# A two-layer encoder trunk: where a filter's spectrum is unfolded, and where its tap sums are multiplied

## The reference

```python
h_full = jnp.concatenate([h[:, 0], zeros((1, n_ch)), h[1:, 1][::-1]], axis=0)
h_full = h_full / jnp.sum(jnp.abs(h_full), axis=0, keepdims=True)
return jnp.fft.rfft(h_full, axis=0).reshape(L + 1, HY_ORDER, W_B)
...
for n, gate in enumerate((x1, x2)):
    z_f = jnp.fft.rfft(z, n=2 * L, axis=1)
    conv = jnp.fft.irfft(z_f * filt_f[:, n], n=2 * L, axis=1)[:, :L]
    z = gate * (conv + bias[n] * z)
```

## Time and profile before

| | |
|---|---|
| median of 3 runs | 2689.77 us (2687.35 to 2689.95) |
| profiled execution | 2684.76 us, of which 2683.2 us are the span |
| PE busy | 2596.8 us (97% of the span) |
| DVE busy | 1862.0 us (69%) |
| ACT busy | 1288.6 us (48%) |
| granted TensorE clock, mean | 0.987 |

### The profile page before, as it was taken

The page is one execution under the profiler, slowest core; times in us unless marked ns, Lnnn a source line. Parts: engine busy times, 40 slices in busy tenths (PEclk is TensorE's granted clock), DMA queues, the critical chain, the costliest instruction groups (busy, mean ns, idle before and its releaser), DMA issues.

```text
span 2683.2 us, 41615 instructions
## 1 busy us (share of the span) xinstructions
PE 2596.8 (97%) x13736; PEld 2157.6 (80%) x13736; DVE 1862.0 (69%) x3251; ACT 1288.6 (48%) x2334; POOL 111.6 (4%) x206
## 2 busy tenths in 40 slices
PE   7999999999999999999989999999999999999998
PEld 6889999976776768898778999898877767688986
DVE  7788778735776767556678878876367757765666
ACT  5555555543444334443465555556344433344535
POOL 2100000000000000000021000000000000000000
PEclk9999999999999999999999999999999999999998
DMA  7544444434443324555564444443344533355554
GB/s 250 164 147 152 152 145 148 157 114 150 150 163 124 128 96 163 187 175 172 165 205 154 152 146 151 148 151 131 138 145 151 173 102 126 102 187 187 173 172 144
DMA packets 115956, 411.83 MB, mean 153 GB/s; under 512 B 15460, under 2 KB 15514, under 8 KB 115584
## 3 DMA queue, kind: packets, MB, share of 16 engines
q1 hardware_dynamic: 107424, 391.17, 43.8%
q0 software_dynamic: 8416, 19.18, 2.2%
HBM read 403.99 MB, written 6.29 MB: 153 GB/s over the span
## 4 chain that ended last, share of the span: by engine, by line
PE 91%; DVE 4%; issue 2%; ACT 2%; DMA 1%; PEldq 0%; PEld 0%; DVEq 0%; POOL 0%; POOLq 0%; ACTq 0%
PE bank L1620 29%; PE bank L1660 19%; PE bank L1662 10%; PE bank L2000 6%; PE bank L1577 5%; PE bank L1595 4%; PE bank L1750 2%; PE bank L1732 2%; PE bank L1713 2%; PE bank L1920 2%; PE bank L1934 1%; PE bank L1818 1%; PE bank L1698 1%; PE bank L1900 1%; PE bank L1842 1%
## 5 line engine op out<-in xcount | busy, mean ns | idle before, releaser
L381 ACT ACTIVATE WH<-ring 128x512 fp32r<-128x512 f32 x1364 | 854.8, 631 | 1176.4 <-PE bank L1620 515.3
L395 DVE TENSOR_TENSOR WL<-ring,WH 128x512 fp32r<-128x512 f32 x852 | 573.3, 688 | 456.2 <-ACT WH L381 454.1
L1660 PE MATMUL bank<-XX,WH 128*128 128x512 f32 x2304 | 820.9, 400 | 27.7 <-DVE XX L564 15.4
L1662 PE MATMUL bank<-XX,WL 128*128 128x256 f32 x2304 | 644.5, 280 | 0.0
L1660 PEld LDWEIGHTS bank<-XX,WH 128*128 128x128 f32 x2304 | 435.7, 189 | 128.5 <-DVE XX L564 15.4
L1620 PE MATMUL bank<-WH,XX 128*128 128x512 f32 x1536 | 493.0, 402 | 4.4 <-issue 3.5
L386 DVE TENSOR_TENSOR WL<-ring,WH 128x512 fp32r<-128x512 f32 x512 | 350.5, 687 | 138.1 <-ACT WH L381 134.0
L1662 PEld LDWEIGHTS bank<-XX,WL 128*128 128x128 f32 x2304 | 437.4, 190 | 0.0
L1620 PEld LDWEIGHTS bank<-WH,XX 128*128 128x128 f32 x1536 | 290.1, 191 | 83.1 <-issue 22.4
L1620 PE MATMUL bank<-WL,XX 128*128 128x512 f32 x768 | 303.6, 395 | 0.0
L1620 PEld LDWEIGHTS bank<-WL,XX 128*128 128x128 f32 x768 | 146.6, 191 | 31.8
(11 more groups left out here) (311 smaller groups left out, 3340.3 us busy)
## 6 DMA issues: line engine op xcount, KB each, us to landing
ring<-in_blocks SPq DMA_DIRECT2D x738, 512.0 KB, 3.3
ARENA<-in_bc POOLq DMA_DIRECT2D x2, 2048.0 KB, 8.6
ARENA<-in_decay POOLq DMA_DIRECT2D x8, 512.0 KB, 4.0
ARENA<-in_x SPq DMA_DIRECT2D x4, 512.0 KB, 8.4
u_scratch<-ARENA POOLq DMA_DIRECT2D x16, 128.0 KB, 2.5
ARENA<-u_scratch POOLq DMA_DIRECT2D x64, 32.0 KB, 3.2
y_scratch<-ARENA POOLq DMA_DIRECT2D x16, 128.0 KB, 2.0
ARENA<-y_scratch POOLq DMA_DIRECT2D x64, 32.0 KB, 2.7
```

The costliest lines, as they stand in the source:

```text
L381: nc.scalar.activation(wh[q], raw(which[0], q), ACT.Copy).then_inc(wh_ready[q], 1)
L395: vec.tensor_tensor(wl[q], raw(which[0], q), wh[q].bitcast(F32), ALU.subtract).then_inc(w_used[slot(which[0], half)], 1)
L1660: ins = mm(bank[b][:, :], h, xx[:, :, k, :], start=(k == 0), stop=(k == DT - 1), skip_group_check=True)
L1662: ins = mm(bank[b][:, 0:T], l, xh[:, k, :], start=False, stop=(k == DT - 1), skip_group_check=True)
```

## The change

It does three things.

- `unfold` is moved on DVE, in slots 2 and 5, from behind the second half of the next block's low parts to between the halves.
- `tap_sums` is moved on PE from slot 8 (behind the forward transform) to slot 6, into the block itself, between its quarters 1 and 2, and writes bank 4 instead of bank 6. Bank 4 held the turned z just before, and holds the first forward transform just after.
- The reciprocal is moved on DVE from slot 8, ahead of the product, to slot 6, behind the second half of the low parts; it now frees bank 4.

```diff
-    "hyc":  [4, 4, 4, 4, 18, 18, 20, 18],
+    "hyc":  [4, 4, 4, 4, 20, 18, 18, 18],
...
-            at = {"taps": 2 * n, "dft": 2 * n + 1, "turn": 4, "fwd": 5 + n, "inv": 7 + n, "sums": 6}[step]
-            return o * 10 + at + (step == "inv" or step == "fwd" and n == 1) if b == 6 else o * 9 + at
+            at = {"taps": 2 * n, "dft": 2 * n + 1, "sums": 5, "turn": 4, "fwd": 5 + n, "inv": 7 + n}[step]
+            return o * 10 + at + (step in ("fwd", "inv")) if b == 4 else o * 9 + at
...
+                    if s_ in (2, 5):
+                        unfold(o, s_ // 3)
                     if s_ in (7, 8, 9):
-                        if s_ == 8:
-                            full(6, "hyc", hyc(o, "sums", 0, 6))
-                            free(v.reciprocal(NS[:, o * 8:o * 8 + 8], bank[6][:, 0:8]), 6)
                         product(o, (0, 1, 1)[s_ - 7], (0, 0, 1)[s_ - 7])
...
-                    if s_ in (2, 5):
-                        unfold(o, s_ // 3)
+                    if s_ == 6:
+                        full(4, "hyc", hyc(o, "sums", 0, 4))
+                        free(v.reciprocal(NS[:, o * 8:o * 8 + 8], bank[4][:, 0:8]), 4)
...
-                def token_block(b, x, j, n, *which):
+                def token_block(b, x, j, n, between, *which):
 
                     for q in range(4):
+                        if q == 2 and between is not None:
+                            between()
...
-                    take_bank(6, "hyc", hyc(o, "sums", 0, 6))
+                    take_bank(4, "hyc", hyc(o, "sums", 0, 4))
...
+                    between = None
                     if s_ == 6:
                         turn_z(o)
+                        between = lambda: tap_sums(o)
...
-                    if s_ == 8:
-                        tap_sums(o)
```

More of the change, by code:

```diff
@@ L356, in split_number, with hyc @@
             return layer * SPLITS + (block_ - skipped + 1) + turn * per
-        def hyc(o, step, n=0, b=4):
-            at = {"taps": 2 * n, "dft": 2 * n + 1, "turn": 4, "fwd": 5 + n, "inv": 7 + n, "sums": 6}[step]
-            return o * 10 + at + (step == "inv" or step == "fwd" and n == 1) if b == 6 else o * 9 + at
+        def hyc(o, step, n, b):
+            at = {"taps": 2 * n, "dft": 2 * n + 1, "sums": 5, "turn": 4, "fwd": 5 + n, "inv": 7 + n}[step]
+            return o * 10 + at + (step in ("fwd", "inv")) if b == 4 else o * 9 + at
         def lift_a(k):
@@ L468, in _ @@
                     if c:
-                        pool.wait_ge(psum_free[7], read_out(layer, "hyc", 7, hyc((c - 1) // 2, "taps", (c - 1) % 2)))
+                        pool.wait_ge(psum_free[7], read_out(layer, "hyc", 7, hyc((c - 1) // 2, "taps", (c - 1) % 2, 7)))
                     else:
@@ L480, in _ @@
                     elif c == 2:
-                        pool.wait_ge(psum_free[7], read_out(layer, "hyc", 7, hyc(0, "inv", 1)))
+                        pool.wait_ge(psum_free[7], read_out(layer, "hyc", 7, hyc(0, "inv", 1, 7)))
                     pool.sem_inc(dec_free, 1)
@@ L983, in even_odd @@
                 def even_odd(o, c):
-                    out_of(7, "hyc", hyc(o, "taps", c))
+                    out_of(7, "hyc", hyc(o, "taps", c, 7))
                     dve.wait_ge(taps_ready, layer * CHUNKS + (o * 2 + c + 1))
                     if c:
-                        full(7, "hyc", hyc(o, "dft", 0))
+                        full(7, "hyc", hyc(o, "dft", 0, 7))
                     f, b = HH[:, 0:2 * CW], HH[:, 2 * CW:4 * CW]
@@ L1637, in token_block, with gated_block @@
                             ins[1].then_inc(parts_used[q], 1)
-                def gated_block(stage, g, p, x, y, *which):
+                def gated_block(stage, g, p, x, y, *which, between=None):
                     b = 0 if p < 4 else 2
@@ L1644, in gated_block @@
                             take_bank(b + t, stage, g)
-                    token_block(b, y if b else x, p - 4 if b else p, 2 if b else 4, *which)
+                    token_block(b, y if b else x, p - 4 if b else p, 2 if b else 4, between, *which)
                 def wide_half(b, half, *which):
@@ L1886, in tap_sums @@
                     pe.wait_ge(sums_ready, layer * CHUNKS + (o * 2 + 2))
-                    take_bank(6, "hyc", hyc(o, "sums", 0, 6))
+                    take_bank(4, "hyc", hyc(o, "sums", 0, 4))
                     for j in range(8):
-                        ins = mm(bank[6][:, j:j + 1], SUM[:, j * P:(j + 1) * P], ones[:, 0:1], start=True, stop=True)
+                        ins = mm(bank[4][:, j:j + 1], SUM[:, j * P:(j + 1) * P], ones[:, 0:1], start=True, stop=True)
                         if j < 7:
                             release(ins)
-                    done(ins, 6)
+                    done(ins, 4)
                 def filter_dft(o, c):
@@ L1959, in _ @@
                         pe.wait_ge(yl_ready, layer * 4 + 2)
-                    gated_block("hyc", k // 6, k % 6, (xh, xl), yc, B_LIFT + 24 + k)
+                    gated_block("hyc", k // 6, k % 6, (xh, xl), yc, B_LIFT + 24 + k, between=between)
                 yb = (split(YBH, WT), split(YBL, WT))
```

## The result

The kernel after takes 2667.11 us (median of 4 runs, 2665.22 to 2670.27), the kernel before in the same session 2689.86 (2687.35 to 2693.46): the ratio is 0.9919 [0.9905, 0.9932]. It is faster by 22.7 us; 2679.1 was predicted, with a range of 2668 to 2693. The profiled executions took 2684.76 us before and 2667.16 after: 17.6 us of difference.

What follows compares the result with a forecast made beforehand. PE, 91% of the chain of waits, was taken as the bound. Waits -8.5, clock -3.2 and registers +1.0 gave -10.7 us: 2674.1 by the profile, plus 5 for the median, 2679.1 us; range 2668 to 2693.

Steps and rivals of the forecast that it cites:

- the low parts behind it stay covered: Slots 2 and 5: low parts delayed by unfold still end about 2 us before PE needs them; cost nothing.
- the sums wait 1.2 us for ACT's copy: Slot 6: PE's sums wait for bank 4 until ACT's first copy of turned z; four times, 4.8 us.
- the transforms 1.6 us for the reciprocal: Before slot 7's forward transforms: PE waits for DVE's reciprocal to free bank 4, 1.66 us each, four times 6.6 us.
- The clock in slot 6: Behind the moved sums TensorE falls to half speed as before in slot 8: 7.5 us, bounds 0 to 20.
- the first rival: Clock stays up, its low stretch cut by full matmuls or falling otherwise in time: -18.2 us, 2671.6 us; chance 0.13.
- Part 1: Slots 2 and 5, unfold ahead of two low parts: gains 13.4 us of waits and 4.5 us of clock.
- 3.4 in four times: Slot 3's taps: PE's wait for DVE, 0.9 us each, was expected to go with the earlier unfold.
- the sum: Whole kernel: -8.5 us of waits, -3.2 of clock, +1.0 of registers, together -10.7 us.
- The 1.4 us of PE's weight loads at L1920: Slot 7's forward transforms: weight loads' wait for the last copy of turned z goes, -1.4 us.
- the margin that was nothing: Slot 9's block: DVE's quarter-2 low part ready about 886.4, wanted 886.5; no cost, bounds 0 to 1 us, four times.
- the signs against the forecast: Reciprocal waits over 3 us, half speed reaching slot 7's transforms, or PE waiting for low parts in slots 6 or 9.
- The registers: PE's instruction list grows by 57 from 254: cost 1.0 us, bounds 0 to 3.5.

Runs made afterwards that it cites:

- the order of groups by itself: Changed kernel with the tap groups issued in bank order 4, 5, 6, 7 instead of 4, 6, 5, 7: 2678.24 us, ratio 0.9964.
- 64 columns in none of four in slot 6: Changed kernel with 64 equal moving columns instead of one in each tap sum, the reciprocal reading every 64th: 2660.68 us, ratio 0.9896.
- in slot 8 of before 64 columns: Kernel before with 64 moving columns instead of one in each tap sum: 2684.71 us, ratio 0.9986.
- the moved sums alone: Changed kernel with unfold put back behind the second half of the low parts; sums and reciprocal stay in slot 6: 2695.31 us, ratio 1.0028.
- the earlier `unfold` with 64 columns: Kernel before with only unfold moved earlier, plus 64 moving columns instead of one in each tap sum: 2655.59 us, ratio 0.9873.

## Why the prediction was wrong in size

**What held.** The earlier `unfold` removes the waits at the turn and the taps, the low parts behind it stay covered, the sums wait 1.2 us for ACT's copy and the transforms 1.6 us for the reciprocal. The clock in slot 6, 7.4 us against 7.5, came out in sum, and partly by luck: two places cost some 2.9 us each, one 1.6 and one nothing. The measured time lies near the first rival, 2671.6, but its mechanism, a clock that stays up, is not what happened.

**The step that failed.** Part 1 priced the taps' wait at what the view of waits gives, "3.4 in four times", 0.9 us each. A stretch of taps got shorter by 2.7 us, and where the clock had also fallen by 4.4. Waiting for bank 6 after bank 4 had been issued parted the two that would have run side by side, and moved all the pairs behind it by one. The trace counted that as busy time. The runs without that wait (the earlier `unfold` alone, or in slot 2 only) have 3.75 us, the one with it (slot 5 only) 6.47, and the order of groups by itself does 1.7 us without any wait. The term is 7.4 us too small (4 x 2.71 = 10.8 us, where 3.4 stood), which is as much as the whole gap of 6.9 us between the profiled difference and the sum; the other errors cancel nearly.

**Smaller terms.** The removed waits elsewhere gave about 0.4 to 0.6 us each more than their recorded idle time: the turn fell by 2.9 us a place against 2.5 recorded, slot 8's transforms and wait from 5.0 to 3.14 against 1.3. With the clock within the sums of slot 8 that is 4.6 us in all beside the earlier trace rows and the price of the clock. The new waits cost 0.2 us each more than recorded (5.5 against 4.8, 7.0 against 6.3). The 1.4 us of PE's weight loads at L1920 are worth some 0.1 us a place at most: slot 7's transforms take 6.57 us where that wait stands (before, and with the earlier `unfold` alone) and 6.46 to 6.48 us in three of four places of the run with the reciprocal between the low parts, where it is gone. Against that, slot 9 costs 0.4 us in each place, within the bounds given for the margin that was nothing; a wait for low parts in slot 9 was also one of the signs against the forecast. The registers cost at most 0.15 us up to the first taps, not 1.0, though in the traces PE executed 1474 register and semaphore instructions where it had executed 1310: 164 more, not 57.

**From the profile to the median.** I added 5 us, since the profiled execution of before lay that far below its median. That of after lies at its median, 2667.16 and 2667.11. So of the 12 us between 2679.1 and 2667.1, 5 are this step and 7 the sum. Each execution has its own falls of the clock, and one profile shows one draw of them: of the 37 runs of before in the sessions of the experiments, the fastest (2684.57) has a mean granted clock of 0.987 and the slowest (2695.74) one of 0.984.

**Open.** What exactly makes the clock fall. Short matmuls beside an idle stretch may have something to do with it: without the idle time there was a fall in none of four places, with 64 columns in none of four in slot 6. But in slot 8 of before 64 columns left three of four, an earlier order of DVE took away two of four with wait and columns unchanged, and a later one (the moved sums alone) two of the changed kernel's three. The Trainium skill, "TensorE: Matmul & The Clock Gate", Part 4, says that a transpose does not count as busy for the clock in the way of other matmuls. That fits the turn, where the fall came in two of four places with the 2.5 us of waits (in three of four with the moved sums alone, in four of four with the early `unfold` in slot 2 only) and in none without them; no run here separates the transposes from the waits.

## What to carry to other kernels

A wait between matmuls that would run side by side costs more than its idle time: look at how the rows of the timeline group (x2 or x4) and compare the whole step with the same step where nothing waits (slot 0's taps, 3.73 us, stood in the same trace). When a step with a wait is to be moved, first ask whether a few microseconds of work that is ready can be put ahead of it where it is: here the sums inside slot 8's block gained a further 10 us (2657.78 to 2647.26), while another bank in another slot gave two waits for one. Price a change with several parts by running each part: one of these two was worth 30 us and the other cost 7.

## What the runs showed that was not expected

**Two 64-row matmuls at once.** Eight passes of a 128-row transform in f32 take 3.03 us; sixteen of the taps, also 512 columns in f32 but with 64 rows, take 3.76, when neighbours use different halves of the rows, and 5.45 when the order leaves two banks without a partner. In the rows of the taps two passes alone take 0.85 or 0.86 us from start to start, and four passes of two banks the same. The Trainium skill, "TensorE: Matmul & The Clock Gate", Part 3, says that several matmuls can run in the array at the same time when each is given its own part of it. The trace agrees, with these 0.86 us for two passes or four; 3.4 us of wait should have been read as 10.8, four times 6.47 - 3.76.

**The spread of the runs may follow the falls.** Kernels whose profile shows no fall in this stage have runs within 0.5 us (64 columns on the changed kernel, 4 runs) and 2.2 us (sums inside slot 8's block, 5 runs). The one with a fall in all eight places, behind each turn and each of slot 8's sums (early in slot 2 only, 5 runs), has 2.3 us. Where some places fall and others not it is 4 to 11 us (3.8 for the earlier `unfold` with 64 columns, 4 runs, 10.9 for the moved sums alone, 9 runs). The counts of runs differ, only one execution of each kernel was profiled, and the clock falls outside this stage too, so this is a pattern and not a cause that was shown.
